# One decoder layer on one core: the score matmuls and the first filler move ahead of the probability transposes, the exponentials ahead of the evacuation

## What is computed

```python
h = x @ w_in + b_in;  qa, ka, va, qb, kb, vb, qc, z = split(h)
oa = banded_causal_attention(rope(qa), rope(ka), va, 127, sinks)  # 8 heads, 2 kv heads, window 128
ob = dilated_attention(rope(qb), rope(kb), vb)   # 4 heads, (w, r) = (128,1), (512,4), (2048,16), merged
oc = memory_attention(qc, mem @ w_mk, mem @ w_mv)                 # 4 heads
y = concat([rms(oa), rms(ob), rms(oc)]) * g_branch * silu(z)
x = layer_norm(alpha * x + y @ w_out) * ln_gain + ln_bias
```

## Time and profile before

| | us |
|---|---|
| median of 3 runs | 533.79 |
| the runs | 529.98, 534.09, 533.79 |
| profiled execution | 535.26 |
| its span | 533.3 |

### The profile page before, as it was taken

One profiled execution on the slowest core, in us unless ns is written; L12 is line 12 of the kernel. 1 busy time (PEld: TensorE's weight loads), 2 busy tenths in 40 slices (PEclk: granted clock), 3 DMA queues, 4 the chain that ended last, 5 costly groups with the idle time before them and its releaser, 6 DMA issues.

```text
span 533.3 us, 9893 instructions
## 1 busy us (share of the span) xinstructions
PE 509.3 (95%) x3560; PEld 469.0 (88%) x3560; DVE 296.1 (56%) x900; ACT 250.0 (47%) x532; POOL 72.7 (14%) x53
## 2 busy tenths in 40 slices
PE   4999999999999979999999989999999999999993
PEld 4999999999999968888888878998889989889982
DVE  4686545466666424434434476665757565565534
ACT  5622212021202045665565588574657465565530
POOL 0000000000000001101111000241414140311415
PEclk9999999999999989999999999999999999999998
DMA  8960553467432443323212576233233324141021
GB/s 291 375 188 13 188 161 111 145 210 216 168 110 80 139 128 110 89 89 101 79 53 91 163 241 214 62 100 97 92 94 91 97 57 139 54 127 41 1 80 79
DMA packets 49743, 66.14 MB, mean 124 GB/s; under 512 B 9248, under 2 KB 39328, under 8 KB 49696
## 3 DMA queue, kind: packets, MB, share of 16 engines
q1 hardware_dynamic: 49120, 64.47, 38.0%
q10 hardware_dynamic: 576, 1.05, 0.6%
HBM read 50.28 MB, written 15.20 MB: 123 GB/s over the span
## 4 chain that ended last, share of the span: by engine, by line
PE 83%; DVE 5%; SPq 4%; DMA 3%; ACT 3%; issue 1%; POOLq 0%; POOL 0%; DVEq 0%; ACTq 0%
PE long_ps L868 15%; PE o_ps L835 11%; PE wide L702 8%; PE wide L700 7%; PE wide L701 7%; PE narrow L817 7%; PE long_ps L777 5%; PE long_ps L778 5%; PE long_ps L779 5%; PE wide L806 4%; PE wide L805 3%; DMA mem_raw<-in_mem_t 2%; ACT prob L1004 1%; SPq L523 1%; PE wide L711 1%; PE wide L713 1%
## 5 line engine op out<-in xcount | busy, mean ns | idle before, releaser
L702 PE MATMUL wide<-x_hi,w_lo 128*128 128x256 f32 x320 | 89.6, 280 | 0.0
L700 PE MATMUL wide<-x_hi,w_hi 128*128 128x256 f32 x320 | 89.4, 279 | 0.2
L701 PE MATMUL wide<-x_lo,w_hi 128*128 128x256 f32 x320 | 89.3, 279 | 0.0
L1004 ACT ACTIVATE prob<-prob,nb 128x256 f32<-128x256 f32 (+7 forms) x96 | 53.0, 583 | 55.7 <-DVE nb L1282 33.3
L1017 ACT ACTIVATE prob_t<-narrow 128x512 f32<-128x512 f32 (+3 forms) x96 | 49.1, 529 | 37.6 <-PE narrow L817 37.2
L949 ACT ACTIVATE spill<-turn 128x512 fp32r<-128x512 f32 x21 | 13.3, 632 | 103.0 <-DVE turn L1162 76.1
L700 PEld LDWEIGHTS wide<-x_hi,w_hi 128*128 128x128 f32 x320 | 59.8, 187 | 0.5 <-issue 0.5
L701 PEld LDWEIGHTS wide<-x_lo,w_hi 128*128 128x128 f32 x320 | 60.2, 188 | 0.0
L702 PEld LDWEIGHTS wide<-x_hi,w_lo 128*128 128x128 f32 x320 | 60.1, 188 | 0.0
L817 PE MATMUL narrow<-ident,prob 128*128 128x128 f32 x328 | 50.7, 279 | 6.9 <-ACT prob L1004 6.5
L1364 POOL TENSOR_TENSOR g_lo<-g_raw,g_hi 128x1024 fp32r<-128x1024 f32 x6 | 14.3, 2387 | 277.1 <-ACT g_hi L954 277.1
(11 more groups left out here) (148 smaller groups left out, 1177.4 us busy)
## 6 DMA issues: line engine op xcount, KB each, us to landing
q_spill<-spill SPq DMA_DIRECT2D x32, 256.0 KB, 2.5
q_pair<-q_spill SPq DMA_DIRECT2D x128, 64.0 KB, 1.9
w_raw<-in_w_qkv SPq DMA_DIRECT2D x12, 512.0 KB, 5.2
x_raw<-in_x_t SPq DMA_DIRECT2D x16, 256.0 KB, 7.9
g_raw<-in_w_gate SPq DMA_DIRECT2D x8, 512.0 KB, 3.5
q_pair<-q_spill SPq DMA_DIRECT2D x32, 128.0 KB, 2.8
q_pair<-q_spill SPq DMA_DIRECT2D x128, 32.0 KB, 1.8
wo_raw<-in_w_out SPq DMA_DIRECT2D x8, 512.0 KB, 4.2
```

The source lines that it names most:

```text
L700: pe.matmul(dst, w_hi[s][:, k, f], t_hi[:, k, cols], start=(k == 0), stop=False)
L701: pe.matmul(dst, w_hi[s][:, k, f], t_lo[:, k, cols], start=False, stop=False)
L702: mm = pe.matmul(dst, w_lo[s][:, k, f], t_hi[:, k, cols], start=False, stop=(k == KT - 1))
L1004: e = act.activation(prob[s][:, cols], src, ACT.Exp, bias=nb[:, r, hh:hh + 1])
```

## The change

Two pieces of code change place. On TensorE the scores of unit v-1 and the first filler part come before the transposes of the probabilities of unit v-2. On ScalarE the exponentials of unit v-1 come before the evacuation of unit v-2. No instruction is added or removed, no buffer and no numbering of turns changes.

```diff
             filler(0, 0)
             for v in range(ITERATIONS):
-                if 0 <= v - 2 < n_units:
-                    transpose_probs(v - 2)
                 if 0 <= v - 1 < n_units:
                     score(v - 1)
                 if v:
                     filler(v, 0)
+                if 0 <= v - 2 < n_units:
+                    transpose_probs(v - 2)
                 for i, j in stage_at(v, Y_AT):
                     transpose_y(i, j)
                 filler(v, 1)
...
+                if 0 <= v - 1 < n_units:
+                    unit_exp(v - 1)
                 if 0 <= v - 2 < n_units:
                     unit_pt(v - 2)
-                if 0 <= v - 1 < n_units:
-                    unit_exp(v - 1)
```

## The result

| | before | after |
|---|---|---|
| median of 4 runs, us | 531.88 | 546.26 |
| the runs, us | 529.50 to 534.09 | 545.89 to 547.28 |
| profiled execution, us | 535.26 | 547.28 |
| its span, us | 533.3 | 545.3 |

The changed kernel is slower: ratio 1.0274, 95% interval 1.0215 to 1.0333. The medians lie 14.4 us apart, the two profiled spans 12.0.

What follows compares the result with a forecast made beforehand. TensorE, busy 95% of the span, was taken as the bound. Span 533.3 + 13.2 (y's waits) + 4.2 (seams) + 6.4 (clock) - 7.5 (gains) = 549.6 us; +16.3 on the median 533.8 gave 550 us, range 540 to 556.

Steps and rivals of the forecast that it cites:

- the three others: Loss 2 (13.2 us), Loss 1 (4.2 us) and the gains (7.5 us off).
- Loss 2: Transposes of y wait in seven iterations for an evacuation queued behind exponentials: 13.2 us, 1.7 to 2.0 each.
- Loss 1: On TensorE, products with v followed directly by scores cost 0.053 us more in 79 iterations: 4.2 us, bounds 0 and 5.
- Gain 1: Probability transposes wait less for exponentials: 3.5 us after 330, 2.0 between 300 and 330, 2.0 at the start, sum 7.5.
- Loss 3: TensorE's clock falls behind four of the seven waits of y, 1.6 us each: 6.4 us, bounds 0 and 11.2.
- my 2.0 us for the start: At the loop's start, products with v of unit 0 finish earlier: gain 2.0 us, bounds 1.0 and 3.3.
- the one near 318: Clock fall near 318, costing about 1.6 us; it may well stay, so half was taken as gain.
- The rival in which y waits and the clock holds: Transposes of y wait as forecast but the clock does not fall: 543.7 us, chance 0.22.

Runs made afterwards that it cites:

- e3: Changed kernel, but ScalarE evacuates before the exponentials in iterations 43, 45, 57, 59, 65, 67, 75: ratio to before 1.0027, span 536.8 us.
- e4: Changed kernel, but TensorE does the second filler part before the transposes of y in the same seven iterations: ratio to before 1.0067, span 536.8 us.
- e2: Changed kernel with TensorE back in the old order, ScalarE still exponentials before evacuation: ratio to before 1.0639, span 563.4 us.
- e9: The kernel of e3 run again in another session: ratio to before 1.0048.
- e7: Kernel before, with TensorE's new order in ten iterations only and b's mask loaded before unit 3's queries: ratio to before 0.9917, span 522.9 us.

## Why the prediction was right, and where its terms were off

**The direction and the range held.** 550 us with 540 to 556 was said, 546.26 measured; +16.3 us was said, +14.4 measured between the medians and +12.0 between the profiled spans. The forecast is nearer to the medians in part by luck: two of the four executions of before had the faster pace. Like with like it was 4 us too high, and that hides more: the clock's term was 5.6 us too high, the three others together 2.1 us too low (the sum below).

**Loss 2, the waits of y: right in mechanism and size.** Seven waits were forecast, 13.2 us together, 1.7 to 2.0 each. The profile has seven, 12.7 us at the matmuls and 14.1 at the weight loads, the longest 2.0 and 2.2. Experiments e3 and e4 show that they are most of the loss: take the queueing away on either engine, in those seven iterations, and 8.5 us of span go. These are 9.0 and 7.9 us of waits and the one fall of the clock (1.6), less what those two executions lost elsewhere (they reached their first scores 1.1 and 0.6 us later, and e3 has the 0.8 us wait for a DMA).

**Loss 1, the seams: right, a little small.** A seam of products with v and scores in the changed kernel:

```profile
470.52 1.00 PE L835 MATMUL o_ps<-v_a,prob_t 128*128 128x66 f32 x8
471.33 0.37 PE L805 MATMUL wide<-k_c,q_pair 128*128 128x256 f32 x1
471.54 0.28 PE L806 MATMUL wide<-k_c,q_pair 128*128 128x256 f32 x1
```

From the start of V to the second score are 1.02 us; the old order's 0.84 to the first transpose and a score's pace of 0.12 make 0.96. Over a stretch in which nothing waits in either kernel, from the scores of iteration 4 to those of iteration 27, before and after:

```profile
198.78 0.31 PE L805 MATMUL wide<-k_b,q_pair 128*128 128x128 f32 x1
...
290.89 0.36 PE L805 MATMUL wide<-k_a,q_pair 128*128 128x256 f32 x1
```

```profile
196.41 0.31 PE L805 MATMUL wide<-k_b,q_pair 128*128 128x128 f32 x1
...
289.88 0.36 PE L805 MATMUL wide<-k_a,q_pair 128*128 128x256 f32 x1
```

92.11 us became 93.47: 1.36 us over 23 iterations, 0.059 each, where I had 0.053 from a filler behind V. Over 79 iterations, if the others cost the same, that is 4.7 us against 4.2.

**Gain 1: too high by about 1 us.** The waits of L817 fell to 4.7 us, where I had said 1 to 3 (3.7 us of them are for exponentials). The start went as worked out (a first wait, then one for unit 1; V of unit 0 at 195.60, or 196.0 when the 0.4 us by which this execution reached its first scores earlier are added, where I had 195.9). After 330 no long wait for exponentials is left, but one of the probability transposes for an evacuation came up (0.67 us at 444.6), the mechanism of loss 2, met by the probability transposes themselves, for which I had not looked. VectorE's maxima were late there: ScalarE began the exponentials 3.9 us after the scores (439.13 to 443.01) and not 2.1 as in iteration 43.

**Loss 3, the clock: the step that failed.** I took four falls behind the seven waits, 6.4 us. The profiled execution has one, and the mean clocks of the other three are 0.995 to 0.997, against 0.993 with the fall; a fall is 0.003, so they had one at most. Of the old kernel's two falls, the one near 189 was inside my 2.0 us for the start, of the one near 318 I had taken half; both went. In the clock alone I had 6.4 - 1.6 - 0.8 = +4.0 us, and the profiles show 1.6 - 3.2 = -1.6. The rival in which y waits and the clock holds, 543.7 us, had this term nearer than the forecast had. The Trainium skill (TensorE: Matmul & The Clock Gate, "Why this matters for your kernels") advises against gaps of more than about 3 us between bursts. By that advice none of the seven waits brings the clock down, as in that rival. A fall behind 1.99 us here, one behind 0.99 us before and four in e2 behind waits of 2.0 to 2.6 us show that it is no safe limit. What separates the wait of iteration 43 (a fall) from the nearly as long ones of 57, 65 and 67 (1.8 to 1.9 us, none) stays open; in e2 the waits of iterations 67 and 75 were equally long (2.6 us), and the clock fell behind the second alone.

**The sum again, with what the profiles show:** 13.8 us of waits on y (start to start), 4.7 of seams and 1.6 for one fall, less 4.1 of waits of probability transposes and 3.2 for two falls, is +12.8 for a measured +12.0; 0.4 of the difference is the earlier first score.

**ScalarE's late evacuations cost nothing for V:** as forecast, no wait of V for an evacuation appears.

## What to carry to other kernels

Before an instruction is put ahead of another on an in-order engine, list who waits for the one that is now second and in which iterations that consumer asks early: here seven iterations of 80 made most of the loss, and without their long waits the new order still cost 0.5% (e9). A ring of two buffers has no slack in the iterations in which one user takes both turns, so that is where to look first. And a wait that is worth 1 us deserves a local remedy: ten reordered iterations, together with an earlier DMA for what they would otherwise have waited for, gained 0.8%, where the uniform reordering pays its seam 79 times.

## What the hardware showed besides

**Two paces of the same projection stage.** Executions of one kernel differ by some 4 us. Before and the kernel with the early mask and ten late transposes, in the same stretch, with TensorE never idle and the clock at full (the count of matmuls is in the brackets):

```profile
100.00:120.00 20.00, 20.00 (x172) 20.00 (x171) 11.04 (x26) 3.79 (x5) 0.00 (x0) 1.00 0.53 174
```

```profile
100.00:120.00 20.00, 20.00 (x179) 20.00 (x178) 12.95 (x30) 4.43 (x6) 0.00 (x0) 1.00 0.55 184
```

172 matmuls of 256 columns against 179; from start to start one takes 118 ns and 113 ns, with the same instructions and the same order. From 68 us to the end of the stage it adds up to 4 us (first scores at 183.3 us in one, at 179.1 in the other). The profiled executions of before, of the changed kernel and of all experiments but e7 and e9 had the slower pace, so the spans compared above, e7's excepted, are not touched. The cause is open; single executions should be compared after a look at this stage.

**How often the clock falls varies between executions.** The kernel before had mean clocks of 0.988 to 0.997 in 25 executions on one chip, that is about none to three falls of 3.4 us; the two that its profile shows are not in every execution. The changed kernel, which has longer waits, had one at most in each of its four.
